# Input tiles of the first down product asked for one row less ahead; sums over features, additions, stores and two rests of weights at other places

## The chip, the cores and the metric

The kernel runs on one core of a Trainium2 chip. The metric is the device time of one execution in microseconds (us); the time before is the median of three executions. Engines are called PE (TensorE, matrix products), ACT (ScalarE), DVE (VectorE), POOL (GpSimd) and SP (SyncE, which here only issues transfers).

## The reference, cut to what matters

One layer of a hybrid block over 1,024 latent tokens of width 1,024, with 256 context tokens: a mixer, and then a SwiGLU network. The change touches the end of the mixer and all of SwiGLU.

```python
D_MODEL, SEQ, CTX_LEN = 1024, 1024, 256
D_FF = 2816                                    # 22 tiles of 128

def rmsnorm(x, g):
    return x * rsqrt(mean(x * x, axis=-1) + 1e-6) * g

def swiglu(h, w_gu, w_down):
    g, u = split(h @ w_gu, 2, axis=-1)
    return (silu(g) * u) @ w_down

y = mixer(rmsnorm(x, g_mix_pre) * (1 + sc_m) + sh_m, ...)
x = x + gt_m * rmsnorm(y, g_mix_post)
h = rmsnorm(x, g_ffn_pre) * (1 + sc_f) + sh_f
x = x + gt_f * rmsnorm(swiglu(h, ffn_w_gu, ffn_w_down), g_ffn_post)
```

All inputs are float32. The kernel keeps that accuracy by splitting each operand into a head (the value rounded to the engine's fp32r format) and a rest (value minus head). A product is then three passes: head by head, head by rest, rest by head.

## The kernel before

Activations lie with features on the 128 partitions and tokens along the row, in two halves of 512 tokens. KT is 8 (tiles of 1,024 features), FT is 22 (tiles of 2,816), NP is 5. A weight tile of 128x1024 is loaded by SP into `raw[:, b]` (b alternates between two buffers). ACT writes its head `w_hi` (line 872, `split` and `head_of`), POOL its rest `w_lo` (line 1363, `rest_of`). These jobs have one numbering through the phases: J_OUT, J_PRE, J_DN, J_D2; `hi_done`, `lo_done` and `job_done` count finished heads, rests and products. A head waits until the product two jobs back is finished (`job_done`), a load until the rest two jobs back is finished (`lo_done`). Each engine takes its instructions strictly in the order written out by hand. SP's order is therefore the order in which transfers are asked for, and a wait in it holds up all later requests.

The phases that matter, in order:

- **Sums over features.** An rmsnorm needs the sum of squares over partitions. DVE adds squares of the 8 tiles into one tile, PE multiplies it with a tile of ones (`sum_over_features(N, acc)`, line 2600; N is 0 to 4), DVE adds epsilon (`variance_of`, line 1992), ACT takes the root (`root`, line 1193), DVE the reciprocal (`inverse_root`, line 1997). Sums 0 and 2 belong to the mixer's output of either half, 1 and 3 to the input of SwiGLU, 4 to the output of SwiGLU for the first half.
- **First products** (J_PRE, `first_half(f, s)`, f = 0 to 21, s = 0 and 1; lines 2656 and 2659). Each f is two half products of 12 matmuls. ACT copies the first out (`first_copy`, line 1234), DVE adds the second to it (`first_sum`, line 2065, into `st2`), and SP stores both to DRAM (`p1_store`, `cg_store`). Meanwhile DVE finishes the second half's mixer output (`add_mixed`), its norm, the scaled input `u1` (line 2124), and prepares four sums of halves (`input_sums`, 2073 to 2078) and their rests (`input_rests`, 2084 and 2086) for the next phase. PE's second half of f waits for `first_sum(f - 2)`, and its first half for `first_copy(f - 2)`.
- **Pair products** (`pair_product(u, r)`, u = 0 to 21, r = 0 to 4; lines 2692 and 2695). Five products of 12 matmuls for each u on sums and differences of weights, which DVE forms (`pair_sums`, lines 2097 to 2102), ACT and POOL split (`pair_head`, `pair_rest`, lines 1257 and 1479). DVE combines the results (lines 2152 to 2177); the gated activations `ab` of both token halves are stored to DRAM in `act_d` (`act_store`).
- **First down product** (J_DN, lines 2716 and 2720), for the first token half. It loops over the 22 rows of `w_down` tiles, i = 0 to 21: row i needs the weight tile `raw` of row i and the activation tile `a0f` of row i, and adds into all 8 banks with 24 matmuls (16 with the head, 8 with the rest of the weight). `rows_dma(i)` loads the weight row (512 KB), `act0_dma(i)` the tile `a0f` (256 KB, two buffers), `act1_dma(i)` the tile `a1f` of the second token half (256 KB, four buffers), which is only split here for later. For each row ACT makes `w_hi`, `a0h` (line 1277) and `a_hi` (1284); POOL makes `w_lo`; DVE makes `a0l` (line 2181) and `a_lo` (2185). PE starts a row on `w_hi` and `a0l`.
- **Second down product** (J_D2, `down_job(k, c)`, lines 2239 and 2244): 8 output tiles k, each of three jobs c. Beside it DVE squares and adds the first half's result (lines 1985 and 1987), then norms it and adds it to x (2198 and 2199); after k = 2 PE waits for that (`n_fin`) and turns it for the output (line 2739). `x1_columns(q)` (line 2759) turns the second half's x.

SP's loop over the rows of the first down product is, before:

```python
for i in range(FT):
    if i + 2 < FT:
        rows_dma(i + 2)          # waits for w_lo of row i
        act1_dma(i + 2)          # from i + 2 = 4: waits for a_lo of row i - 2
        if i + 4 < FT:
            act0_dma(i + 4)      # waits for a0l of row i + 2
```

Of the kernel before, what the change touches and what calls it, by code (L numbers as in the profile page):

```python
# [19 lines left out]
ALU = mybir.AluOpType  # L20
# [27 lines left out]
E_OUT = 0  # L48
# [116 lines left out]
def program(nc, A, out):  # L165
    ctx = ExitStack()
    with ctx:
# [366 lines left out]
        def _(sp):  # L534
# [206 lines left out]
            def rows_dma(i):  # L741

                sp.wait_ge(lo_done, J_DN + i - 1)
                sp.dma_start(raw[:, i % 2, :], w_dn[:, i, :]).then_inc(raw_ld[i % 2], 16)
# [6 lines left out]
            def cg_store(f):  # L751

                sp.wait_ge(c_eva, C_EVA0 + f + 1)
                sp.dma_start(cg_d[f], st2[:, f % 2, :]).then_inc(cg_out[f % 2], 16)
# [31 lines left out]
            def act0_dma(i):  # L786

                if i >= 2:
                    sp.wait_ge(a0_lo, A0_LO0 + i - 1)
                sp.wait_ge(a_out[0], A_OUT0 + 16 * (i + 1))  # L790
                sp.dma_start(a0f[:, i % 2, :], act_d[0, i]).then_inc(a0_ld[i % 2], 16)

            def act1_dma(i):

                if i < 4:
                    sp.wait_ge(a_ok, A_OK0 + 2 * FT)
                else:
                    sp.wait_ge(a1_lo, A1_LO0 + i - 3)
                sp.wait_ge(a_out[1], A_OUT0 + 16 * (i + 1))
                sp.dma_start(a1f[:, i % 4, :], act_d[1, i]).then_inc(a1_ld[i % 4], 16)  # L800
# [3 lines left out]
            sp.wait_ge(n_x1, KT)  # L804
            sp.dma_start(x1_d, x1h[0][:].rearrange("p k n -> p (k n)")).then_inc(x1_out, 16)
            for f in range(FT):
                if f + 2 < FT:
                    gate_dma(f + 2)
                else:
                    rows_dma(f + 2 - FT)  # L810
                p1_store(f)
                if f >= 2:
                    cg_store(f - 2)
                if f in (15, 17):
                    pair_dma((f - 15) // 2)
            cg_store(FT - 2)
# [3 lines left out]
            for u in range(FT):  # L820
                if 1 <= u < FT - 1:
                    first_dma(u + 1)
                if u + 2 < FT:
                    pair_dma(u + 2)
                if u:
                    act_store(u - 1, 1)
                if u in (2, 3):
                    act0_dma(u - 2)
                if u == FT - 1:
                    act0_dma(2)  # L830
                    act0_dma(3)
                act_store(u, 0)
            act_store(FT - 1, 1)
            act1_dma(0)
# [2 lines left out]
            for i in range(FT):  # L837
                if i + 2 < FT:
                    rows_dma(i + 2)
                    act1_dma(i + 2)  # L840
                    if i + 4 < FT:
                        act0_dma(i + 4)
                else:
                    raw_dma(i % 2, J_DN + i + 2, src_d(i + 2 - FT))
                if i in (4, 6, 8, 10):
                    c = (i - 4) * KT * HALF // 8
                    sp.dma_start(x1h[0][:].rearrange("p k n -> p (k n)")[:, c:c + KT * HALF // 4],
                                 x1_d[:, c:c + KT * HALF // 4]).then_inc(x1_ld, 16)
# [17 lines left out]
        def _(act):  # L866
# [369 lines left out]
            def input_sums(j):  # L1236

                for r in (0, 1, 2, 3):
                    act.wait_ge(t_sum, T_SUM0 + 4 * j + r + 1)
                    act.activation(t_hi[r][:, j, :], tsum[:, j % 2, r, :], ACT.Copy).then_inc(th_ok, 1)  # L1240
                act.wait_ge(u_ok, U_OK0 + KT)
                act.activation(t_hi[4][:, j, :], u1[:, 4 + j, :], ACT.Identity, bias=mod[:, 28 + j, 0:1]).then_inc(th_ok, 1)
# [36 lines left out]
            def act1_head(i):  # L1279

                act.wait_ge(a1_ld[i % 4], A1_LD0 + 16 * (i // 4 + 1))
                if i == 0:
# [2 lines left out]

            chain = {1: lambda: root(2), 3: lambda: x1_squares(1, range(1)), 4: lambda: x1_squares(1, range(1, 4)),
                     5: lambda: x1_squares(1, range(4, 8)), 6: lambda: root(3), 10: lambda: input_sums(1),
                     11: lambda: input_sums(2), 12: lambda: input_sums(3)}
            for f in range(FT):
                head_of(J_PRE + f + 1)  # L1290
                if f in chain:
# [67 lines left out]
        def _(pool):  # L1359
# [8 lines left out]
            def rest_of(J):  # L1368
                rest(0, J - J % 2, J % 2)
# [116 lines left out]
            for u in range(FT):  # L1486
                if u:
                    for r in range(NP):
                        pair_rest(u, r)
                if u in (1, 2):  # L1490
                    rest_of(J_DN + u - 1)
            for j in range(2, FT + 24):
                rest_of(J_DN + j)

# [2 lines left out]
        def _(dve):  # L1497
# [543 lines left out]
            def mixed_squares(ks):  # L2041

                for k in ks:
                    dve.wait_ge(acc_free, E_OUT + KT + k + 3)
                    link(dve.tensor_tensor(yacc[:], sq1[:, 0, :] if k == 1 else yacc[:], sq1[:, k, :], ALU.add))

            mixed_squares(range(1, 4))
            rstd_of(1)
            for k in range(KT + 1):
                if k < KT:  # L2050
                    ffn_input(k)
                if k in (1, 2):
                    mixed_squares(range(k + 3, k + 4))
                if k:
                    ffn_rest(k - 1)

# [44 lines left out]
                dve.wait_ge(s_ok, S_OK0 + 4 * u + 3)  # L2101
                dve.tensor_tensor(s4[:], g[:, HALF:D], s2[:], ALU.subtract).then_inc(s_ok, 1)

            mixed_squares(range(6, KT))
            dve.nop().then_inc(n_sum, 1)
            link(dve.tensor_tensor(dsh[:], mod[:, 24:28, 0], mod[:, 28:32, 0], ALU.subtract))
            first_sum(0)
            variance_of(2)
            inverse_root(2)
# [9 lines left out]
            first_sum(5)  # L2119
            variance_of(3)  # L2120
            inverse_root(3)
            first_sum(6)
            for k in range(KT):
                dve.scalar_tensor_tensor(u1[:, k, :], x1h[1][:, k, :], affn[:, k:k + 1], rstd[:], ALU.mult, ALU.mult).then_inc(u_ok, 1)
                if k == 4:
                    first_sum(7)
            input_sums(0)
            first_sum(8)
            input_sums(1)
            first_sum(9)  # L2130
            input_rests(0)
            input_sums(2)
            first_sum(10)
            input_rests(1)
            input_sums(3)
            first_sum(11)
            input_rests(2)
            first_sum(12)
            input_rests(3)
            for f in range(13, FT):  # L2140
                first_sum(f)
                if f == 18:
                    pair_sums(0)
# [87 lines left out]
        def _(pe):  # L2231
# [412 lines left out]
            def first_half(f, s):  # L2644

                b, J, dst = f % 2, J_PRE + f, ps[:, 4 * s + f % 2, :]
                if f >= 2:
                    pe.wait_ge(c_eva if s else p1_ev, (C_EVA0 if s else P1_EV0) + f - 1)
                elif s == 0:
                    pe.wait_ge(acc_free, E_OUT + 16 + 2)  # L2650
                pe.wait_ge(hi_done, J + 1)
                for k in range(4 * s, 4 * s + 4):
                    if f == 0:
                        pe.wait_ge(n_hl, k + 1)
                    for x in (hb_hi, hb_lo):
                        pe.matmul(dst, w_hi[:, b, k * P:(k + 1) * P], x[:, k, :], start=k == 4 * s and x is hb_hi, stop=False)  # L2656
                pe.wait_ge(lo_done, J + 1)
                for k in range(4 * s, 4 * s + 4):
                    ins = pe.matmul(dst, w_lo[:, b, k * P:(k + 1) * P], hb_hi[:, k, :], start=False, stop=k == 4 * s + 3)  # L2659
                ins.then_inc(job_done if s else p1_ps, 1)  # L2660

            x_turns(range(KT, KT + 3))
            for f in range(FT):
                first_half(f, 0)
                if f == 1:
                    sum_over_features(2, yacc)
                if f in (3, 4):
                    x_turns(range(2 * f + 6, 2 * f + 7))
                first_half(f, 1)
                if f in (2, 3, 4):  # L2670
                    x_turns(range(2 * f + 7, 2 * f + 8))
                if f == 5:
                    sum_over_features(3, nrm)

            def pair_product(u, r):
# [94 lines left out]
            for k in range(KT):  # L2770
                for c in range(3):
                    down_job(k, c)
                    if k == 0 and c == 0:
                        pe.wait_ge(y0_a, Y0_A0 + 4)
                        pe.wait_ge(y0_d, Y0_D0 + 4)
                        x1_columns(0)
                        x1_columns(1)
                    if k == 0 and c == 2:
                        sum_over_features(4, nrm)
                if k == 0:  # L2780
                    pe.wait_ge(t_ev, 2)
                    x1_columns(2)
                    x1_columns(3)
                else:
                    pe.wait_ge(t_ev, 4 if k < 5 else 8)
                    down_columns(k - 1)
                if k == 2:
                    pe.wait_ge(n_fin, 1)
                if 2 <= k < 6:
                    if k > 2:  # L2790
                        pe.wait_ge(o_ev, k - 2)
                    output_turns(k - 2)
# [32 lines left out]
```

## Time and profile before

| | us |
|---|---|
| median of three executions | 1476.96 (1475.63 to 1481.14) |
| profiled execution, its time | 1478.04 |
| its span in the trace | 1476.2 |
| PE busy (matmuls) | 1372.9, 93% of the span |
| DVE busy | 954.9, 65% |
| POOL busy | 596.0, 40% |
| ACT busy | 574.2, 39% |
| moved by DMA | 195.73 MB, mean 133 GB/s |

The profiled execution's time is 1.8 us above its span: start and end lie outside the trace. A busy PE means that matmuls are in flight; it can be busy at half its clock. "L2716" is line 2716 of the kernel. "[2.69 <-DVE a0l L2181]" behind an instruction says that its engine was idle for 2.69 us before it, and that DVE's instruction of line 2181 on tile a0l released it. DVEq and PEq stand for an engine's sequencer, SPq for SP's transfer requests.

### The profile page before, as it was taken

What the parts mean: (1) busy time and instruction counts of PE and PEld (TensorE: products, weight loads), DVE (VectorE), ACT (ScalarE), POOL (GpSimd) and SP (SyncE); (2) the same over time, 40 slices, a digit from 0 to 9 for tenths busy, and PEclk for the clock granted to TensorE, in tenths of its full rate; (3) what the DMA queues carried; (4) which work ended last, traced back from release to release, by engine and by line L of the source; (5) the groups of instructions that cost most, each with busy time, mean ns of one, the idle gap of its engine ahead of it and who ended that gap; (6) DMA issues with size and microseconds to landing.
All of it is one profiled execution on the core that took longest, in us unless ns stands there. A gap on an engine that the chain in (4) does not pass through costs nothing.

```text
span 1476.2 us, 19347 instructions
## 1 busy us (share of the span) xinstructions
PE 1372.9 (93%) x7489; PEld 1113.6 (75%) x7489; DVE 954.9 (65%) x1230; ACT 574.2 (39%) x954; POOL 596.0 (40%) x333
## 2 busy tenths in 40 slices
PE   5999998999998999999999999999999776788997
PEld 1589667999887888887777878888888655567886
DVE  6774558884918887459987387777786332346522
ACT  5662653322216778535434422333332222233221
POOL 3363112161428552663433565455552222233442
PEclk9999999999999999999999999999999988899998
DMA  9852113214105445444446745544552434342342
GB/s 324 320 165 64 41 43 103 69 44 142 30 17 140 137 137 145 143 144 141 139 147 205 236 142 157 171 150 143 165 164 77 139 128 141 122 138 68 102 133 87
DMA packets 219910, 195.73 MB, mean 133 GB/s; under 512 B 13043, under 2 KB 179329, under 8 KB 219563
## 3 DMA queue, kind: packets, MB, share of 16 engines
q1 hardware_dynamic: 217827, 187.51, 40.5%
q10 hardware_dynamic: 1992, 6.99, 1.3%
q8 instruction: 59, 0.97, 0.3%
q14 instruction: 32, 0.26, 0.1%
HBM read 160.88 MB, written 33.98 MB: 132 GB/s over the span
## 4 chain that ended last, share of the span: by engine, by line
PE 65%; DVE 17%; DMA 6%; ACT 4%; issue 3%; SPq 1%; POOL 0%; DVEq 0%; ACTq 0%
PE ps L2692 13%; PE ps L2407 11%; PE ps L2695 6%; PE ps L2239 6%; DMA raw<-in_ffn_w_down 6%; PE ps L2412 6%; DVE a0l L2181 3%; PE ps L2244 3%; PE ps L2656 2%; PE ps L2570 2%; PE ps L2547 2%; PE ps L2508 2%; PE ps L2425 1%; PE ps L2659 1%; DVE nrm L2017 1%
## 5 line engine op out<-in xcount | busy, mean ns | idle before, releaser
L1363 POOL TENSOR_TENSOR w_lo<-raw,w_hi 128x1024 fp32r<-128x1024 f32 x84 | 207.8, 2474 | 345.7 <-ACT w_hi L872 345.7
L872 ACT ACTIVATE w_hi<-raw 128x1024 fp32r<-128x1024 f32 x84 | 88.9, 1058 | 254.7 <-DMA raw<-in_ffn_w_down 131.7
L1383 POOL TENSOR_TENSOR w_lo<-raw,w_hi 128x1024 fp32r<-128x1024 f32 x21 | 88.6, 4219 | 219.1 <-ACT w_hi L1017 219.1
L2692 PE MATMUL ps<-t_hi,whi 128*128 128x512 f32 x440 | 171.4, 390 | 3.3 <-DVE ym L2154 3.3
L2692 PE MATMUL ps<-t_lo,whi 128*128 128x512 f32 x440 | 171.2, 389 | 0.0
L1479 POOL TENSOR_TENSOR wlo<-wsum,whi 128x512 fp32r<-128x512 f32 x88 | 123.0, 1400 | 111.9 <-ACT whi L1257 111.9
L2407 PE MATMUL ps<-ha_hi,w_hi 128*128 128x512 f32 (+2 forms) x432 | 162.6, 377 | 3.1 <-ACT p_hy L1024 2.8
L2407 PE MATMUL ps<-ha_lo,w_hi 128*128 128x512 f32 (+2 forms) x432 | 160.3, 371 | 0.0
L2181 DVE TENSOR_TENSOR a0l<-a0f,a0h 128x512 fp32r<-128x512 f32 x20 | 49.0, 2448 | 114.7 <-ACT a0h L1277 114.7
L2716 PE MATMUL ps<-a0h,w_hi 128*128 128x512 f32 x176 | 80.5, 458 | 45.2 <-DVE a0l L2181 45.2
L2695 PE MATMUL ps<-t_hi,wlo 128*128 128x512 f32 x440 | 117.6, 389 | 0.0
L1257 ACT ACTIVATE whi<-wsum 128x512 fp32r<-128x512 f32 x88 | 55.5, 632 | 148.9 <-PE ps L2695 120.1
L2412 PE MATMUL ps<-ha_hi,w_lo 128*128 128x512 f32 (+2 forms) x432 | 99.1, 371 | 0.0
L2692 PEld LDWEIGHTS ps<-t_hi,whi 128*128 128x128 f32 x440 | 82.6, 188 | 21.2 <-DVE ym L2154 4.1
L2695 PEld LDWEIGHTS ps<-t_hi,wlo 128*128 128x128 f32 x440 | 82.6, 188 | 17.1
L2692 PEld LDWEIGHTS ps<-t_lo,whi 128*128 128x128 f32 x440 | 82.6, 188 | 17.1
L2407 PEld LDWEIGHTS ps<-ha_hi,w_hi 128*128 128x128 f32 x432 | 81.1, 188 | 17.1 <-issue 3.2
L2407 PEld LDWEIGHTS ps<-ha_lo,w_hi 128*128 128x128 f32 x432 | 81.1, 188 | 10.2
L2412 PEld LDWEIGHTS ps<-ha_hi,w_lo 128*128 128x128 f32 x432 | 80.0, 188 | 10.3
L2716 PEld LDWEIGHTS ps<-a0h,w_hi 128*128 128x128 f32 x176 | 39.3, 224 | 61.4 <-issue 52.7
L2656 PE MATMUL ps<-hb_hi,w_hi 128*128 128x512 f32 x176 | 73.0, 415 | 6.2 <-DVE st L2065 3.6
L2716 PE MATMUL ps<-a0l,w_hi 128*128 128x512 f32 x176 | 78.2, 444 | 0.0
(348 smaller groups left out, 3029.6 us busy)
## 6 DMA issues: line engine op xcount, KB each, us to landing
raw<-in_ffn_w_gu SPq DMA_DIRECT2D x66, 512.0 KB, 5.6
raw<-in_ffn_w_down SPq DMA_DIRECT2D x38, 512.0 KB, 3.8
ada1x<-in_ada_w SPq DMA_DIRECT2D x32, 512.0 KB, 4.0
raw<-in_w_in SPq DMA_DIRECT2D x22, 512.0 KB, 4.0
act_d<-ab SPq DMA_DIRECT2D x44, 256.0 KB, 2.4
ada<-in_ada_w SPq DMA_DIRECT2D x4, 2048.0 KB, 21.7
raw<-in_w_out SPq DMA_DIRECT2D x16, 512.0 KB, 3.7
p_d<-st SPq DMA_DIRECT2D x22, 256.0 KB, 2.1
```

Source lines behind the costliest of these rows:

```text
L872: act.activation(w_hi[:, b, :], raw[:, b, :], ACT.Copy).then_inc(hi_done, 1)
L1363: pool.tensor_tensor(w_lo[:, b, :], raw[:, b, :], w_hi[:, b, :].bitcast(F32), ALU.subtract).then_inc(lo_done, 1)
L1383: pool.tensor_tensor(w_lo[:, b, :], raw[:, b, :], w_hi[:, b, :].bitcast(F32), ALU.subtract).then_inc(llo, 1)
L1479: pool.tensor_tensor(wlo[r][:], src, whi[r][:].bitcast(F32), ALU.subtract).then_inc(wl_ok, 1)
L2181: dve.tensor_tensor(a0l[:, (i + 1) % 2, :], a0f[:, (i + 1) % 2, :], a0h[:, (i + 1) % 2, :].bitcast(F32), ALU.subtract).then_inc(a0_lo, 1)
L2239: pe.matmul(dst, w_hi[:, b, k * P:(k + 1) * P], x, start=start and i_ == 0 and n == 0, stop=False)
L2407: pe.matmul(dst, w_hi[:, b, k * P:(k + 1) * P], x[:, k, a:z], start=k == 0 and n == 0, stop=False)
L2412: ins = pe.matmul(dst, w_lo[:, b, k * P:(k + 1) * P], ha_hi[:, k, a:z], start=False, stop=k == KT - 1)
L2656: pe.matmul(dst, w_hi[:, b, k * P:(k + 1) * P], x[:, k, :], start=k == 4 * s and x is hb_hi, stop=False)
L2692: pe.matmul(dst, whi[r][:, j * P:(j + 1) * P], x[:, j, :], start=j == 0 and x is t_hi[r], stop=False)
L2695: ins = pe.matmul(dst, wlo[r][:, j * P:(j + 1) * P], t_hi[r][:, j, :], start=False, stop=j == 3)
L2716: pe.matmul(ps[:, m, :], w_hi[:, b, m * P:(m + 1) * P], x[:, b, :], start=i == 0 and x is a0h, stop=False)
```

## The change

Seven edits of order; no instruction of arithmetic is added or removed.

1. In SP's loop over rows of the first down product, `act0_dma(i + 4)` at the end of an iteration becomes `act0_dma(i + 3)` between `rows_dma` and `act1_dma`. `act0_dma(3)` before the loop goes.
2. In the first products SP stores `st2` of f - 2 (`cg_store`) at the start of iteration f, no longer behind `gate_dma(f + 2)` and `p1_store(f)`.
3. POOL makes the rests of weights of rows 0 and 1 of the first down product after the pair products' rests, no longer within u = 1 and u = 2.
4. PE takes sum 3 after f = 6 (before: after f = 5), and sum 4 after job (k = 1, c = 0) (before: after job (k = 0, c = 2)).
5. f = 0 waits for one finished copy of the mixer's output less.
6. DVE adds squares 4 and 5 of the second half, and forms `dsh`, at other places; the sums of inputs and `first_sum` are interleaved otherwise, from f = 6 to 14.
7. ACT takes the heads of input sums 2 and 3 at f = 12 and 14 (before: 11 and 12).

```diff
--- before.py
+++ after.py
@@ -804,13 +804,13 @@
             sp.wait_ge(n_x1, KT)
             sp.dma_start(x1_d, x1h[0][:].rearrange("p k n -> p (k n)")).then_inc(x1_out, 16)
             for f in range(FT):
+                if f >= 2:
+                    cg_store(f - 2)
                 if f + 2 < FT:
                     gate_dma(f + 2)
                 else:
                     rows_dma(f + 2 - FT)
                 p1_store(f)
-                if f >= 2:
-                    cg_store(f - 2)
                 if f in (15, 17):
                     pair_dma((f - 15) // 2)
             cg_store(FT - 2)
@@ -828,7 +828,6 @@
                     act0_dma(u - 2)
                 if u == FT - 1:
                     act0_dma(2)
-                    act0_dma(3)
                 act_store(u, 0)
             act_store(FT - 1, 1)
             act1_dma(0)
@@ -837,9 +836,9 @@
             for i in range(FT):
                 if i + 2 < FT:
                     rows_dma(i + 2)
+                    if i + 3 < FT:
+                        act0_dma(i + 3)
                     act1_dma(i + 2)
-                    if i + 4 < FT:
-                        act0_dma(i + 4)
                 else:
                     raw_dma(i % 2, J_DN + i + 2, src_d(i + 2 - FT))
                 if i in (4, 6, 8, 10):
@@ -1285,7 +1284,7 @@
 
             chain = {1: lambda: root(2), 3: lambda: x1_squares(1, range(1)), 4: lambda: x1_squares(1, range(1, 4)),
                      5: lambda: x1_squares(1, range(4, 8)), 6: lambda: root(3), 10: lambda: input_sums(1),
-                     11: lambda: input_sums(2), 12: lambda: input_sums(3)}
+                     12: lambda: input_sums(2), 14: lambda: input_sums(3)}
             for f in range(FT):
                 head_of(J_PRE + f + 1)
                 if f in chain:
@@ -1487,8 +1486,8 @@
                 if u:
                     for r in range(NP):
                         pair_rest(u, r)
-                if u in (1, 2):
-                    rest_of(J_DN + u - 1)
+            rest_of(J_DN)
+            rest_of(J_DN + 1)
             for j in range(2, FT + 24):
                 rest_of(J_DN + j)
 
@@ -2044,13 +2043,12 @@
                     dve.wait_ge(acc_free, E_OUT + KT + k + 3)
                     link(dve.tensor_tensor(yacc[:], sq1[:, 0, :] if k == 1 else yacc[:], sq1[:, k, :], ALU.add))
 
-            mixed_squares(range(1, 4))
+            mixed_squares(range(1, 5))
+            link(dve.tensor_tensor(dsh[:], mod[:, 24:28, 0], mod[:, 28:32, 0], ALU.subtract))
             rstd_of(1)
             for k in range(KT + 1):
                 if k < KT:
                     ffn_input(k)
-                if k in (1, 2):
-                    mixed_squares(range(k + 3, k + 4))
                 if k:
                     ffn_rest(k - 1)
 
@@ -2101,9 +2099,8 @@
                 dve.wait_ge(s_ok, S_OK0 + 4 * u + 3)
                 dve.tensor_tensor(s4[:], g[:, HALF:D], s2[:], ALU.subtract).then_inc(s_ok, 1)
 
-            mixed_squares(range(6, KT))
+            mixed_squares(range(5, KT))
             dve.nop().then_inc(n_sum, 1)
-            link(dve.tensor_tensor(dsh[:], mod[:, 24:28, 0], mod[:, 28:32, 0], ALU.subtract))
             first_sum(0)
             variance_of(2)
             inverse_root(2)
@@ -2119,25 +2116,27 @@
             first_sum(5)
             variance_of(3)
             inverse_root(3)
-            first_sum(6)
             for k in range(KT):
                 dve.scalar_tensor_tensor(u1[:, k, :], x1h[1][:, k, :], affn[:, k:k + 1], rstd[:], ALU.mult, ALU.mult).then_inc(u_ok, 1)
                 if k == 4:
-                    first_sum(7)
+                    first_sum(6)
+            first_sum(7)
             input_sums(0)
             first_sum(8)
             input_sums(1)
             first_sum(9)
             input_rests(0)
+            first_sum(10)
             input_sums(2)
-            first_sum(10)
+            first_sum(11)
             input_rests(1)
+            first_sum(12)
             input_sums(3)
-            first_sum(11)
+            first_sum(13)
             input_rests(2)
-            first_sum(12)
+            first_sum(14)
             input_rests(3)
-            for f in range(13, FT):
+            for f in range(15, FT):
                 first_sum(f)
                 if f == 18:
                     pair_sums(0)
@@ -2647,7 +2646,7 @@
                 if f >= 2:
                     pe.wait_ge(c_eva if s else p1_ev, (C_EVA0 if s else P1_EV0) + f - 1)
                 elif s == 0:
-                    pe.wait_ge(acc_free, E_OUT + 16 + 2)
+                    pe.wait_ge(acc_free, E_OUT + 16 + f + 1)
                 pe.wait_ge(hi_done, J + 1)
                 for k in range(4 * s, 4 * s + 4):
                     if f == 0:
@@ -2669,7 +2668,7 @@
                 first_half(f, 1)
                 if f in (2, 3, 4):
                     x_turns(range(2 * f + 7, 2 * f + 8))
-                if f == 5:
+                if f == 6:
                     sum_over_features(3, nrm)
 
             def pair_product(u, r):
@@ -2775,7 +2774,7 @@
                         pe.wait_ge(y0_d, Y0_D0 + 4)
                         x1_columns(0)
                         x1_columns(1)
-                    if k == 0 and c == 2:
+                    if k == 1 and c == 0:
                         sum_over_features(4, nrm)
                 if k == 0:
                     pe.wait_ge(t_ev, 2)
```

## Rows read from the trace of the kernel before

**Rows 1.** Stretches: us; busy time of PE, PEld, DVE, ACT, POOL; clock; DMA share; GB/s.
```profile
788.00:837.00 49.00, 47.94 (x203) 39.23 (x204) 20.52 (x24) 19.87 (x27) 26.47 (x13) 0.97 0.78 240
...
1151.00:1327.00 176.00, 130.80 (x483) 100.81 (x481) 63.92 (x43) 43.67 (x64) 48.99 (x21) 0.88 0.39 130
```

**Rows 2.** PE's waits from 600 us on: waiter, releaser, us in total, times, longest.
```profile
PE ps L2716 <- DVE a0l L2181: 45.2, 18, 5.0
PE ps L2600 <- DVEq L2118: 5.0, 1, 5.0
PE ps L2600 <- DVEq L2193: 4.2, 1, 4.2
...
PE ps L2692 <- DVE ym L2154: 3.3, 2, 1.6
```

**Rows 3.** Timeline of all engines, one row of the first down product: start, us, what.
```profile
1153.38 0.42 SPq L744 DMA_DIRECT2D raw<-in_ffn_w_down  x1
...
1157.36 1.06 ACT L872 ACTIVATE w_hi<-raw 128x1024 fp32r<-128x1024 f32 x1 [6.33 <-DMA raw<-in_ffn_w_down]
...
1158.49 2.35 POOL L1363 TENSOR_TENSOR w_lo<-raw,w_hi 128x1024 fp32r<-128x1024 f32 x1 [6.06 <-ACT w_hi L872]
...
1158.97 2.42 DVE L2181 TENSOR_TENSOR a0l<-a0f,a0h 128x512 fp32r<-128x512 f32 x1 [5.39 <-ACT a0h L1277]
...
1161.42 0.32 SPq L791 DMA_DIRECT2D a0f<-act_d  x1
...
1161.54 0.77 PE L2716 MATMUL ps<-a0h,w_hi 128*128 128x512 f32 x1 [2.69 <-DVE a0l L2181]
```

**Rows 4.** Timeline of PE: starts of rows 0, 1 and 2, and the end.
```profile
1140.44 0.39 PE L2716 MATMUL ps<-a0h,w_hi 128*128 128x512 f32 x1
...
1145.88 0.39 PE L2716 MATMUL ps<-a0h,w_hi 128*128 128x512 f32 x1
...
1153.12 0.47 PE L2716 MATMUL ps<-a0h,w_hi 128*128 128x512 f32 x1 [1.64 <-DVE a0l L2181]
...
1326.95 0.39 PE L2720 MATMUL ps<-a0h,w_lo 128*128 128x512 f32 x1
```

**Rows 5.** Transfers from 1140 to 1330 us: count, KB each, median us to landing.
```profile
raw<-in_ffn_w_down SPq DMA_DIRECT2D x22, 512.0 KB, 3.9
a1f<-act_d SPq DMA_DIRECT2D x22, 256.0 KB, 4.1
a0f<-act_d SPq DMA_DIRECT2D x18, 256.0 KB, 2.7
```

**Rows 6.** Timeline of PE in the first products.
```profile
740.09 2.07 PE L2600 MATMUL ps<-nrm,ones 128*128 128x512 f32 x2 [4.96 <-DVEq L2118]
...
788.51 0.50 PE L2656 MATMUL ps<-hb_hi,w_hi 128*128 128x512 f32 x1 [2.77 <-DVE st L2065]
...
836.43 1.07 PE L2659 MATMUL ps<-hb_hi,w_lo 128*128 128x512 f32 x4
```

**Rows 7.** Timeline of DVE in the pair products.
```profile
853.61 2.88 DVE L2097 TENSOR_TENSOR wsum<-raw 128x512 f32<-128x512 f32 x1
...
859.45 0.67 DVE L2152 TENSOR_TENSOR px<-px,ps 128x512 f32<-128x512 f32 x1
```

**Rows 8.** Timeline of POOL, pair products and start of the first down product.
```profile
857.29 4.61 POOL L1479 TENSOR_TENSOR wlo<-wsum,whi 128x512 fp32r<-128x512 f32 x3 [1.35 <-ACT whi L1257]
...
1150.06 2.37 POOL L1363 TENSOR_TENSOR w_lo<-raw,w_hi 128x1024 fp32r<-128x1024 f32 x1 [21.01 <-ACT w_hi L872]
```

**Rows 9.** Timeline of PE in the second down product.
```profile
1342.89 1.52 PE L2244 MATMUL ps<-a_hi,w_lo 128*128 128x512 f32 x6
...
1356.69 1.98 PE L2244 MATMUL ps<-a_hi,w_lo 128*128 128x512 f32 x8
...
1384.23 1.09 PE L2739 MATMUL ps<-ident,x1a 128*128 128x128 f32 x8 [0.16 <-DVEq L2200]
```

**Rows 10.** Timeline of DVE in the second down product.
```profile
1360.38 3.35 DVE L1997 RECIPROCAL rstd<-nrm 128x512 f32<-128x512 f32 x1 [9.44 <-ACT nrm L1193]
```

## The prediction

> **What bounds the kernel now.** I read the page first: PE has the most busy time, but a share over the whole span hides stages. So next came the windows by stage. In the first down product (1151 to 1327 us) PE is busy for only 130.80 of 176 us, at a granted clock of 0.88, while DMA works 39% of its time; in the first products just before (788 to 837 us) PE is nearly always busy, at 0.97 [rows 1]. Then the list of PE's waits: 45.2 us go to `a0l` of DVE in that stage, and four smaller sums elsewhere are touched by the diff [rows 2]. The chain of waits names, in that stage, the same three things again and again: the load of `raw`, `a0l`, the load of `raw`. Last, the timeline of one row shows why [rows 3].
>
> There the reader should see one closed loop. SP asks for the weight tile at 1153.38. ACT starts its head at 1157.36, DVE's `a0l` runs from 1158.97 to 1161.39, and only at 1161.42 does SP go on, with the request for `a0f`; the next weight tile comes right behind it. SP stands at `act0_dma(i + 4)`, which waits for `a0l` of row i + 2, and that row's weights were asked for only in the same iteration. So a weight tile is requested, carried, split and used before the next is requested: one in flight, though there are two buffers. Rows 0 and 1, prefetched, follow each other after 5.44 us (1140.44 to 1145.88). From the start of row 2 to the end of row 21 PE needs 1153.12 to 1327.2, so 174.1 us for 20 rows, 8.70 each [rows 4].
>
> **The first down product.** After the change iteration i asks for weights i + 2, then `a0f` of i + 3, which waits for `a0l` of row i + 1. That row's weights were requested one iteration earlier. The loop stays, but now it spans two rows. Its length: landing, then the 4.2 us from ACT's head to PE's start (1157.36 to 1161.54) [rows 3]. The landing grows, because the request for a weight tile now stands behind `a0f` and `a1f`. Before, the last of the same three requests, `a1f`, starts about 0.9 us after the first and lands in 4.1 us: 5.0 us for the 1 MB [rows 5]. With that, two rows take at least 5.0 + 4.2 = 9.2 us, 4.6 each. That is below PE's 5.44, so PE becomes the bound. Second loop: a head waits for the product two rows back, and 4.2 us later its row is ready, while PE works 5.44 us on the row between; 1.2 us are left. ACT's three splits, DVE's two and POOL's one take at most 3.1 us a row, hidden under 5.44. Moved past each other on SP: `a1f` now stands behind the wait for `a0l`, but has four buffers and is not needed by PE here. Four iterations also load 512 KB of x; a landing 1.7 us longer would make that pair of rows 10.9 us, just PE's 10.88, so I cost it at nothing in the sum and at 5 us in the range.
>
> Bandwidth: 1.05 MB in 5.44 us is 193 GB/s; 788 to 837 us moves 240 GB/s for 49 us with PE hardly waiting [rows 1].
>
> Row 2's start stays as it is, since its weights are asked for behind the stores of the last activations, in the same place as before. So 20 rows x 5.44 = 108.8, plus 0.4 for its slow clock: 109.2 instead of 174.1. **Gain 64.9 us.**
>
> On the length of a transfer, the Trainium skill ("DMA: Bandwidth & Descriptors", section "Anatomy of one DMA") fits, for transfers that GpSimd issues, about 2.0 us plus bytes over 436 GB/s. An estimate by that page for the 1 MB would be 4.4 us; the rows give 5.0 for requests of SP, and I use the rows. By either, PE stays the bound and the sum is the same.
>
> **The first products.** PE waits 4.96 us for sum 3 and starts it at 740.09, so the sum's input was ready then [rows 6]. The idle began at 735.13; f = 6, put in the gap, takes 5.44 and ends at 740.6, so the sum finds its input ready and DVE's chain behind it loses nothing. The whole price is larger than the idle: from 735.1 to the end of f = 21 (837.5) PE takes 102.4 us for 16 x 5.44 + 0.9 (the sum) = 87.9 of work, a loss of 14.5. It holds the 4.96, a wait for `first_sum` (2.77 at 788.51) [rows 6] and matmuls at half clock behind these. What comes back: `first_sum(6)` now stands behind five tiles of `u1`. I count sum 0.9, root and reciprocal 4.7, five tiles and the addition 6 with one stall: it is done near 751, when PE, at f = 8, would want it at 749.5: 1.4 us. From there DVE does sums or rests, 3.0 us, an addition, 0.6, and one stall of 2.1 behind POOL (2.88 less 0.7 to 0.8) per f, about 5.7 against PE's 5.44, over eight f: 2 us less a slack of 1. I give back 2.5. Squares, `dsh` and the earlier start of f = 0 move things by under 1 us either way; `cg_store` first only blocks SP if `first_sum(f - 2)` is later than PE's first half of f - 1, and then `gate_dma(f + 2)` and `p1_store(f)` wait behind it; with a load needed 10 us later, cost nothing. I add 0.5 for f = 0. **Gain 12.5 us** (bounds: 5, when most of the idle comes back at f = 8 to 16; 15, when none does).
>
> **The pair products.** In u = 1 and 2 POOL works on a rest of 128x1024 while DVE wants two inputs from SBUF: L2097 takes 2.88 us, where `px`, with as many elements, takes 0.67 [rows 7], and PE waits 3.3 us for `ym` [rows 2]. Without these rests, with the slow matmuls behind each wait: **gain 3.7 us**. The two rests go into POOL's idle time before 1150.06, 21.01 us long [rows 8]. They take 2.4 us each, from 1129.05 to 1133.8, and are needed at 1144 by the tail of row 0; without that cover they would cost 4.8. DVE combines u = 21 at that time. It need not suffer: `px` took 0.67 us at 859.45 inside POOL's 4.61 us stretch from 857.29 [rows 7, 8]. That instruction has one input in PSUM.
>
> By the Trainium skill ("SBUF — State Buffer", section "Who interferes with whom"), DVE and GpSimd block each other when DVE reads two inputs from SBUF, and not with at most one. The trace agrees, 2.88 against 0.67 us. If every DVE instruction were blocked, PE would wait some 0.3 us in u = 21, and the sum would be 0.3 smaller.
>
> **The second down product.** PE waits 4.2 us for the input of sum 4 [rows 2]. Job 2 ends at 1344.3 and job 3 at 1358.5, 14.2 us [rows 9], for a sum (0.9), 16 transposes (1.8) and a job (5.44), 8.1 at full clock. With the sum last, the wait is filled. Is the chain behind it late? No: the root stood in ACT's queue behind the head that waits for job 3, so the reciprocal started at 1360.38, after an idle of 9.44 us [rows 10], though the sum was long done. Afterwards it starts 0.9 (sum) + 1.6 (epsilon, root) after job 3, not 1.9: so 0.6 later after job 3. But PE, too, now has the sum (0.9) between job 3 and its wait for `n_fin`, which was 0.16 us [rows 9] and doesn't grow; it rises by up to 2 us if one more DVE instruction falls under one of POOL. **Gain 6.0 us.**
>
> **Sum.** 64.9 + 12.5 + 3.7 + 6.0 = 87.1, from 1478.04 (span 1476.2 and 1.8 around it): 1390.9. The profiled execution was 1.1 above the median, so 1390.
>
> **Rivals.**
> - *Carriage is late (10%).* If a weight tile behind two others lands after 8.5 us, not 5.0, two rows take 12.7, 6.35 each: 18 us less gain, 1408. For it: x's loads, and ACT's head waiting 6.33 us for landings now. Against: 240 GB/s was held.
> - *DVE becomes late in the first products (10%).* Most of the idle comes back at f = 8 to 16 (the bound of 5 in place of 12.5) and the chain to `n_fin` adds 2: 9.5 us less, 1399. For it: 5.7 us of DVE against 5.44 of PE per f. Against: before, the same work had one wait of PE of 2.77 us for it [rows 6].
> - *The request does not help (4%).* Were the row's 8.70 us set by something other than SP's wait, only the other parts count: 22.2 us, 1455. Against: SP resumes 0.03 us after `a0l` [rows 3].
> - *Transfers of one queue go one after another (2%), slower.* A row then needs 3.9 + 2.7 + 4.1 = 10.7 us [rows 5], 40 us more over 20 rows, less 22.2: 1495. It decides from 9.8 us a row on. Against: the three are requested within 0.9 us and have all landed after 5.0.
>
> By the Trainium skill ("DMA: Bandwidth & Descriptors", section "Queues, rings and completion order"), descriptors of one ring start in order and a later one may complete before an earlier one; it speaks against the last rival, and the trace agrees.
>
> **Chances.** My forecast 0.74; the rivals 0.10, 0.10, 0.04, 0.02. They give 1390, 1408, 1399, 1455, 1495. The range reaches to 1405 and down to 1384 (no idle given back, f = 0 starting earlier, median lower). Within 0.5% is about what a measurement of this kernel can tell from no change: 0.01; slower 0.02; faster 0.97.
>
> **What would show it.** Right: about 5.44 us from row to row, SP asking for `a0f` while the weights of the next row are in flight, ACT waiting for PE and not for landings, clock 1.00 there; sum 3 and sum 4 without idle before them; no long L2097 in u = 1 and 2. Wrong: ACT's heads still wait for `raw`; rows above 6 us; new waits of PE for `first_sum` at f = 8 to 16; a wait for `n_fin` of several us.

## The result and the profile after

| | median us (lowest to highest) | runs |
|---|---|---|
| before | 1479.05 (1475.63 to 1483.78) | 4 |
| after | 1408.08 (1403.66 to 1411.31) | 4 |
| ratio | 0.9516, 95% interval 0.9473 to 0.9559 | |

The kernel became 4.8% faster, some 71 us. I had forecast 1390 with a range of 1384 to 1405, so the gain came, but smaller than the range allows: the median lies 18 us above the forecast. The profiled execution of after took 1403.66 us, 74.4 less than that of before (the forecast for this pair was 87.1); the working below is made between these two.

The stretches of the profile after that answer to [rows 1] (us; busy time of PE, PEld, DVE, ACT, POOL; clock; DMA share; GB/s):

```profile
786.00:835.00 49.00, 43.38 (x184) 35.14 (x183) 25.62 (x27) 18.91 (x27) 23.42 (x12) 0.97 0.71 221
1146.00:1259.00 113.00, 109.57 (x479) 89.64 (x480) 64.21 (x43) 43.70 (x63) 49.54 (x21) 1.00 0.59 198
```

The first down product now has PE busy for 97% at a clock of 1.00, where it was 74% at 0.88. The stretch of the first products before it, which had looked full, is now the poorer one: 43.38 of 49 us.

PE's waits after, which answer to [rows 2]:

```profile
PE ps L2655 <- ACT w_hi L871: 5.6, 1, 5.6
PE ps L2655 <- DVE hb_lo L2026: 2.7, 6, 0.6
PE ps L2715 <- DVE a0l L2180: 2.4, 3, 1.7
PE ps L2599 <- DVEq L2103: 1.8, 1, 1.8
PE ps L2715 <- ACT w_hi L871: 1.3, 1, 1.3
PE ps L2655 <- DVE st L2063: 0.9, 1, 0.9
```

The 45.2 us for `a0l` are 2.4, and the waits for sums 3 and 4 and for `ym` are gone. Three waits have no counterpart before: 5.6 us for a head of weights in the first products, 1.8 for sum 2, and 1.3 for a head of weights at row 13 of the first down product. The 2.7 us for `hb_lo` stand where 2.5 for `yo` stood, at the start of f = 0.

One row of the first down product in the profile after, SP, ACT and DVE, against [rows 3]:

```profile
1225.62 0.32 SPq L791 DMA_DIRECT2D a0f<-act_d  x1
1226.03 0.38 SPq L800 DMA_DIRECT2D a1f<-act_d  x1
1226.46 0.42 SPq L744 DMA_DIRECT2D raw<-in_ffn_w_down  x1
```
```profile
1226.94 1.06 ACT L871 ACTIVATE w_hi<-raw 128x1024 fp32r<-128x1024 f32 x1 [3.34 <-PE ps L2719]
```
```profile
1228.55 2.48 DVE L2180 TENSOR_TENSOR a0l<-a0f,a0h 128x512 fp32r<-128x512 f32 x1 [2.36 <-ACT a0h L1276]
```

The reader should compare two things with before. ACT's head here no longer waits for the load but for PE's product two rows back (so do 14 of 21 heads from row 2 on; the heads of rows 2, 3, 7, 9, 11, 13 and 14 still wait for their load). And it starts 0.5 us after a request for weights, so it cannot be using that tile: its own was asked for earlier. The end of row 21 follows the start of row 2 (1147.43) after 111.9 us, 5.59 a row.

Where the 74.4 us came from, stage by stage in the two profiles. A stage begins and ends with an instruction that both have:

| stretch | before | after | gain | forecast |
|---|---|---|---|---|
| start to the turn of x ahead of f = 0 | 693.27 | 694.95 | -1.7 | 0 |
| from there to the first pair product | 144.1 | 140.5 | 3.5 | 12.5 |
| pair products | 303.1 | 299.2 | 3.9 | 3.7 |
| rows 0 and 1 of the first down product | 12.7 | 12.8 | -0.1 | 0 |
| rows 2 to 21 | 174.1 | 111.9 | 62.2 | 64.9 |
| second down product, to the end | 149.0 | 142.6 | 6.4 | 6.0 |

The hole is in the first products: 9.0 of the 12.7 us that this execution lacks.

### The profile page after: what moved, and what is told of

It reads as the page before. It is cut to its first block, busy times and chain, and to the rows that moved or that the text cites. A ratio compares the mean times of both kernels' runs of the same rounds, so it can differ in the third digit from the quotient of the medians.

```text
span 1401.9 us, 19347 instructions
## 1 busy us (share of the span) xinstructions
PE 1345.7 (96%) x7489; PEld 1098.0 (78%) x7489; DVE 955.8 (68%) x1230; ACT 572.9 (41%) x954; POOL 596.2 (43%) x333
## 4 chain that ended last, share of the span: by engine, by line
PE 77%; DVE 11%; ACT 4%; issue 2%; DMA 2%; SPq 0%; DVEq 0%; ACTq 0%
PE ps L2691 14%; PE ps L2406 12%; PE ps L2238 8%; PE ps L2694 7%; PE ps L2411 6%; PE ps L2243 4%; PE ps L2715 3%; PE ps L2655 3%; PE ps L2569 2%; DMA raw<-in_ffn_w_down 2%; PE ps L2719 2%; PE ps L2546 2%; PE ps L2507 1%; PE ps L2658 1%; PE ps L2424 1%
## 5 line engine op out<-in xcount | busy, mean ns | idle before, releaser
L2715 PE MATMUL ps<-a0h,w_hi 128*128 128x512 f32 x176 | 68.9, 392 | 3.7 <-DVE a0l L2180 2.4
L2238 PE MATMUL ps<-a_hi,w_hi 128*128 128x512 f32 x176 | 69.9, 397 | 0.0
L1443 POOL TENSOR_TENSOR tb<-gt,mask 128x288 f32<-128x288 f32 (+1 forms) x48 | 52.6, 1125 | 39.8 <-DVE amin L1957 38.3
```

The costliest lines, as they stand in the source:

```text
L2238: pe.matmul(dst, w_hi[:, b, k * P:(k + 1) * P], x, start=start and i_ == 0 and n == 0, stop=False)
L2715: pe.matmul(ps[:, m, :], w_hi[:, b, m * P:(m + 1) * P], x[:, b, :], start=i == 0 and x is a0h, stop=False)
```

## The experiments

The runs came in three groups, and each group timed the kernel before beside them. Medians of one kernel differ by up to 2.5 us between groups, so a kernel is set against others of its group where it can be.

**First group: what each part is worth, and what stands behind PE's new wait.** The timelines of after around that wait, SP, ACT, PE and DVE:

```profile
794.55 0.60 SPq L749 DMA_DIRECT2D p_d<-st  x1
802.98 1.01 SPq L765 DMA_DIRECT2D raw<-in_ffn_w_gu  x2
804.03 1.03 SPq L754 DMA_DIRECT2D cg_d<-st  x1
805.10 0.43 SPq L560 DMA_DIRECT2D raw<-in_ffn_w_gu  x1
```
```profile
811.05 1.06 ACT L871 ACTIVATE w_hi<-raw 128x1024 fp32r<-128x1024 f32 x1 [10.94 <-DMA raw<-in_ffn_w_gu]
```
```profile
812.25 0.77 PE L2655 MATMUL ps<-hb_hi,w_hi 128*128 128x512 f32 x1 [5.62 <-ACT w_hi L871]
```
```profile
800.07 2.88 DVE L2084 SCALAR_TENSOR_TENSOR t_lo<-u,mod,t_hi 128x512 fp32r<-128x512 f32 x1
```

Read it from below: PE waits for ACT's head, the head for a load, and the load was asked for late. DVE's last rest of the input sums ends at 802.95. Only then does SP send L765, the first request of weights for the pair products (`pair_dma(0)`), which stands after f = 15 and waits for exactly these rests. Behind it in SP's order stand a store and, at 805.10, the weights of f = 18 (L560). They travel behind 1 MB, so ACT gets them at 811.05 and PE stands for 5.62 us. SP's waits name it: 

```profile
SPq L765 <- DVE t_lo L2084: 7.8, 1, 7.8
```

The kernel before has no such wait. The same rest and the same request there:

```profile
796.56 2.88 DVE L2086 SCALAR_TENSOR_TENSOR t_lo<-u,mod,t_hi 128x512 fp32r<-128x512 f32 x1
```
```profile
802.79 1.21 SPq L765 DMA_DIRECT2D raw<-in_ffn_w_gu  x2
```

The last rest was finished at 799.44, 3.3 us before SP came to the request.

E1, the changed kernel again, as the mark. 

> The changed kernel again, unaltered, as the mark for the other runs of this call. If the spread of its four runs so far (1403.7 to 1411.3) belongs to the kernel, its median lies near 1408 and single runs differ by several us; if the runs above 1410 were chance of the chip, it lies near 1404.

Measured: 1406.03 us (1403.48 to 1408.49), ratio to before 0.9504 (0.948 to 0.9528). Single runs differ by 5 us, as those of the kernel before in this group do (1477.11 to 1482.39). PE's waits for `a0l` are 5.1 us in this profile against 2.4, and rows 0 to 21 take 126.3 us against 124.6: a part of the spread lies in that stage.

E2, the kernel before with the first edit alone:

```diff
-                    act1_dma(i + 2)
-                    if i + 4 < FT:
-                        act0_dma(i + 4)
+                    if i + 3 < FT:
+                        act0_dma(i + 3)
+                    act1_dma(i + 2)
```

> The kernel before with one edit: a0f of row i + 3 asked for ahead of a1f of row i + 2 (and no a0f of row 3 before the loop). Theory: this edit carries nearly the whole gain, 62 us as the traces of before and after show for this stage: 1415 to 1419, PE 112 us from row 2 to the end of row 21. Rival (the stage's gain came with the other edits, which moved the phase of the engines to one another): less than 50 us, above 1427.

Measured: 1416.98 us, ratio 0.9589 (0.956 to 0.9618), 61.8 us less than before in the same group, of the 72.8 of E1. This edit carries most of the gain by itself, and PE's waits for `a0l` are 4.8 us in its profile.

E3, the changed kernel without that edit. 

> The changed kernel with the request of a0f as before (one row more ahead, at the end of an iteration). Theory: what is left is the pair products (3.8), the second down product (6.5) and about 3.7 of the first products, 14 us: 1463 to 1467. Rival (the other edits are worth 22 us, as I predicted, and the first down product is what fell short): 1455 to 1458.

Measured: 1466.07 us, ratio 0.9917 (0.9893 to 0.994), 12.7 us less than before. The rest of the diff is worth 13 us, not the 22 of my forecast, and its profile has the same 5.6 us of waiting for a head. So the hole is not in the first down product.

E4, the changed kernel with the pair requests two products later:

```diff
-                if f in (15, 17):
-                    pair_dma((f - 15) // 2)
+                if f in (17, 19):
+                    pair_dma((f - 17) // 2)
```

> The changed kernel with the two requests of weights for the pair products after f = 17 and 19, not 15 and 17. Theory: PE's 5.6 us before f = 18 come from SP standing at the first of them until the last rest of the input sums is there (802.87), with the weights of f = 18 asked for behind it. Then the wait and its slow matmuls go: 7 us less than the changed kernel in the same call, SP's wait for t_lo 0 to 1 us. Rival (the transfers of 1 MB themselves hold up the weights of f = 18, wherever they stand): the same wait of about 5 us of PE two products later, at f = 20, and no change beyond 1 us.

Measured: 1398.26 us (1394.97 to 1398.79), ratio 0.9444 (0.9422 to 0.9466), 7.8 us less than E1. SP's timeline and PE's waits in E4:

```profile
804.65 1.79 SPq L765 DMA_DIRECT2D raw<-in_ffn_w_gu  x2
...
808.60 0.43 SPq L560 DMA_DIRECT2D raw<-in_ffn_w_gu  x1
```
```profile
PE ps L2715 <- DVE a0l L2180: 4.1, 3, 2.8
PE ps L2655 <- DVE hb_lo L2026: 2.7, 6, 0.6
PE ps L2599 <- DVEq L2103: 1.9, 1, 1.9
PE ps L2655 <- DVE st L2063: 0.9, 1, 0.9
```

The same 1 MB stands in the same way ahead of the weights of f = 20, but the request doesn't wait, and PE has no wait for a head. So it was the wait in SP's queue, not the transfer: the rival is out.

**Second group: the other parts one by one.** E5, the kernel before with sum 3 after f = 6 (`if f == 5` becomes `if f == 6`). 

> The kernel before with one edit: sum 3 after f = 6. Theory: PE's 5.0 us of waiting for it go, with the slow matmuls behind: 6 to 7 us less, near 1472. PE, now earlier, may wait longer for first_sum at f = 9 to 14, where DVE's order is still the old one: 2.8 us there could become up to 8, and then little is gained (1476 to 1479). Rival: the idle is the sum's own price, and moves with it to f = 7.

Measured: 1472.79 us, ratio 0.9958 (0.9942 to 0.9973), 6.9 us less. The wait of 5.0 is gone, and it doesn't reappear; PE's waits for `first_sum` are 4.0 us, as against 3.6 before. The feared growth didn't come. From the turn of x to the first pair product PE takes 138.4 us, 5.7 less than before.

This run also tells something about SP's wait. PE is earlier here, but DVE's order is the old one, and SP does not wait at the pair request:

```profile
794.40 2.88 DVE L2086 SCALAR_TENSOR_TENSOR t_lo<-u,mod,t_hi 128x512 fp32r<-128x512 f32 x1
```
```profile
799.75 1.63 SPq L765 DMA_DIRECT2D raw<-in_ffn_w_gu  x2
```

Counted from the turn of x ahead of f = 0 (693.27 before, 696.51 in E5, 694.95 after), the last rest ends at 106.2, 100.8 and 108.0 us, and SP comes to the request at 109.5, 103.2 and 100.2. With sum 3 moved, PE and the rests come earlier together, and no wait arises; against E5 the changed kernel has SP 3.0 us earlier and, by its new order of DVE's work, the rests 7.2 us later.

E6, the kernel before with sum 4 after job (k = 1, c = 0) and the two rests of weights behind the pair products. 

> The kernel before with two edits far apart: sum 4 after job (k = 1, c = 0), and the rests of weights of rows 0 and 1 behind the pair products. Theory: 6.0 to 6.5 us in the second down product and 3.7 in the pair products, 10 us: 1468 to 1469, no wait of PE for the input of sum 4, none for ym, the wait for n_fin under 1 us. Rival (the norm behind sum 4 is later by the 5.4 us of a job and PE stands at n_fin): 1473 or more, a wait of about 5 us at the turn of x.

Measured: 1468.16 us, ratio 0.9924 (0.9907 to 0.994), 11.6 us less by medians (10.8 between the two profiled spans). DVE and PE there, against [rows 9, 10]:

```profile
1349.63 3.35 DVE L1997 RECIPROCAL rstd<-nrm 128x512 f32<-128x512 f32 x1 [0.70 <-ACT nrm L1193]
```
```profile
1373.50 1.04 PE L2739 MATMUL ps<-ident,x1a 128*128 128x128 f32 x8
```

The reciprocal had waited 9.44 us for the root; now 0.70. PE turns x without a wait before it: a sum one job later did not make the norm late.

E7, E4 with squares 4 and 5 at their old places (`dsh` stays early):

```diff
-            mixed_squares(range(1, 5))
+            mixed_squares(range(1, 4))
...
+                if k in (1, 2):
+                    mixed_squares(range(k + 3, k + 4))
...
-            mixed_squares(range(5, KT))
+            mixed_squares(range(6, KT))
```

> The kernel with pair requests after f = 17 and 19, and DVE's squares 4 and 5 of the second half back at their old places (4 and 5 inside the loop over ffn_input, 6 and 7 behind it); dsh stays early. Theory: of the first products' missing gain 2 us lie in the squares: three of them behind the loop meet two rests of POOL, and sum 2 waits 1.9 us. Then the sum's input is ready 2 us earlier, PE's wait for it is under 0.5 us, and the whole is 1.5 to 2.5 us shorter. Rival: the delay is that of the chain ahead of the loop (one square and dsh more before the root), or of PE's clock after its early start at f = 0: then the wait stays, and nothing is gained or some is lost.

Measured: 1397.16 us (1394.35 to 1398.96), ratio 0.9447 (0.9433 to 0.9461); against 1398.26 in another group that shows nothing by itself, and E8 below, of this group and without this edit, is no slower (1396.54). The times alone do not show a gain; the profiles do. From the turn of x ahead of f = 0 to the first pair product E4 takes 133.5 us and E7 131.0, and PE has no wait for sum 2. From that turn to sum 2 all five profiles without this edit (after, E1, E3, E4, E8) take 15.9 to 16.0 us, and all five with it (E7 and E9 to E12) 13.6 or 13.7. DVE and POOL in after, and DVE in E7:

```profile
704.51 6.27 DVE L2044 TENSOR_TENSOR yacc<-yacc,sq 128x512 f32<-128x512 f32 x3
```
```profile
704.76 5.47 POOL L1362 TENSOR_TENSOR w_lo<-raw,w_hi 128x1024 fp32r<-128x1024 f32 x2 [8.30 <-ACT w_hi L871]
```
```profile
702.93 3.49 DVE L2044 TENSOR_TENSOR yacc<-yacc,sq 128x512 f32<-128x512 f32 x2
```

Three additions left for the end fall on two rests of POOL back to back, and take 6.27 us for 2.1 of work; of two left for the end, one is held up, and they take 3.49.

E8, E4 with the four loads of x in iterations 4, 8, 12 and 16 (slices as before). 

> The kernel with pair requests after f = 17 and 19, and the four loads of x (512 KB each) in iterations 4, 8, 12 and 16 of the first down product, not 4, 6, 8 and 10. Theory: four loads two rows apart fall on the weights of rows of the same parity, the loop over two rows is then over 10.9 us long, and PE waits for a0l near rows 7 to 13; four rows apart each delay is made good before the next. PE's waits for a0l go from 4.1 us to the 1.7 to 2.8 at row 2, 1.5 to 2.5 us less. Rival: the waits come from transfers as such: the same waits, further apart.

Measured: 1396.54 us (1393.9 to 1400.06), ratio 0.9444 (0.9426 to 0.9462): no difference from E4 that these runs can tell. My expectation that only the wait at row 2 would be left was wrong: 3.4 us in all, of which 1.75 at row 2; behind it 1.6 in four waits, where E4 has 1.3 in two. The four waits are at rows 7, 11, 15 and 19, whose weights are the next request behind a load of x. Each load of x has its wait, further apart. The rival holds.

**Third group: the length of the burst.** The mark is E7 again. 

> The kernel with pair requests after f = 17 and 19 and squares 4 and 5 at their old places, unaltered, as the mark for the other three of this call: about 1396, PE 124 to 126 us from the start of row 0 to the end of row 21 of the first down product (22 rows at 5.44 are 119.7).

Measured: 1394.68 us (1392.78 to 1398.34), 123.3 us for the 22 rows in the profile, 1.6 us of waits for `a0l` and 1.3 for a head. The same kernel as E7 had 126.2 us and 5.3 us of waits for `a0l`, so one profile of this stage is no measure of 2 or 3 us.

E10, the mark with the loads of x behind weights 2 to 5 of the second down product. 

> The mark with the four loads of x asked for in the second down product (one behind each of the weights 2 to 5), none in the first. Theory: without x a weight tile lands 6.0 us after the first of its three requests, the loop over two rows is 10.2 us, under PE's 10.88, and PE has no wait for a0l behind row 2; the stage takes about 122 us, 3 to 4 less than the mark. Rival: transfers are late without x too, and PE's waits for a0l stay above 3 us; or the loads of x now come too late for the norm's end, and a wait for n_fin of several us takes the gain.

Measured: 1392.05 us (1390.61 to 1393.96), ratio 0.9405 (0.9389 to 0.942). PE's waits in this stage:

```profile
PE ps L2717 <- DVE a0l L2182: 2.7, 1, 2.7
```

It is the one at row 2. The waits behind it are gone, and rows 3 to 21 take 5.44 us each, PE's own time; so they do in E11 and E12. In E9 these rows take 2.1 us more and in E7 4.6 more. Transfers without x are in time. But the stage as a whole is no shorter than the mark's (124.2 us, and about 123.5 in E11 and E12), where I had expected 122. Row 2 started 1.4 us later after row 0 than in the mark, and then ran slowly:

```profile
1139.20:1146.27 7.07, 7.07 (x24) 5.73 (x25) 3.83 (x3) 0.44 (x1) 2.08 (x1) 0.77 0.78 266
```

The granted clock in it is 0.77; in the mark row 2 takes 5.56 us at 1.00. E4, E11 and E12 have the slow row 2 too (7.1 us), E1, E2, E7 and E8 don't. Why is open: E1 waited 2.3 us just before a quick row 2, E11 only 1.9 before a slow one. By medians 2.6 us are gained; the ranges overlap.

E11, the mark with `act1_dma(i + 2)` ahead of `act0_dma(i + 3)`. 

> The mark with a1f of row i + 2 asked for ahead of a0f of row i + 3, so ahead of SP's wait for a0l. Theory (position within the iteration matters only through the length of the burst): a1f goes out earlier, the burst behind the wait is 0.75 MB, not 1 MB, weights land 0.8 us sooner after the wait, and PE's waits for a0l fall from 5.3 to 2 to 4 us: 1 to 3 us less. Rival: the place ahead of a1f is what the gain needs; then rows take longer than 5.44 us and the whole is several us more.

Measured: 1393.09 us (1392.3 to 1393.54), ratio 0.9416 (0.94 to 0.9432). PE waits 1.9 us for `a0l`, at row 2 alone, and a load of weights takes 4.4 us at the median, not 5.0. So `a0f` asked for one row less ahead is what counts; its place ahead of `a1f` isn't needed. By medians the new place is worth 1.6 us, with ranges that overlap.

E12, both. 

> The mark with both edits: loads of x in the second down product, and a1f ahead of a0f. Theory: the two are one cure for the same lateness, so this is no better than the better of them by more than 1 us: about 1392 to 1394, PE's only wait for a0l that at row 2. Rival (they add): 3 us below either.

Measured: 1392.21 us (1391.87 to 1394.24), ratio 0.9412 (0.9396 to 0.9429), as expected no better than either. These three are the best versions run, some 14 us below the changed kernel's 1406.03 of another group; they are not told apart by these runs.

## Why the prediction was right and wrong

**The first down product: right in mechanism, 2.7 us off in size.** One tile in flight was the limit, and PE became the bound. The mis-sized term is x: "I cost it at nothing in the sum". What went before it was the landing. I put "5.0 us for the 1 MB", from `a1f`, which stood last. After, the weights stand last; transfers of the profile after, against [rows 5]:

```profile
raw<-in_ffn_w_down SPq DMA_DIRECT2D x22, 512.0 KB, 5.1
a1f<-act_d SPq DMA_DIRECT2D x22, 256.0 KB, 3.2
a0f<-act_d SPq DMA_DIRECT2D x19, 256.0 KB, 2.8
```

From the first request (1225.62) to that for weights pass 0.84 us, and 5.1 more to the landing: 5.9, so a loop over two rows of 10.1 instead of 9.2. That is still under 10.88 and costs nothing by itself, but it leaves 0.8 us, where I had counted on 1.7. The four tiles asked for right behind a load of x (rows 7, 9, 11 and 13) landed after 7.0, 5.9, 5.7 and 7.0 us, and PE waited 0.47, 0.23, 0 and 1.30 us at these rows. With the slower matmuls behind the waits, rows 3 to 21 take 3.0 us more than 5.44 each. E10 to E12 show that this goes in either of two ways: x elsewhere, or fewer bytes ahead of the weights.

**The first products: the step that failed.** "Gain 12.5 us (bounds: 5, when most of the idle comes back at f = 8 to 16; 15, when none does)" became 3.5, below my lower bound. The parts I looked at came as worked out: sum 3 has no idle before it and its edit alone gives 6.9 us (E5); PE's one wait for `first_sum`, at f = 8, is 0.9 us, for which I had given back 1.4; f = 9 to 16 have no wait, for which I had given back 1. I had compared DVE with PE alone. What I left out is another reader of DVE's work: `pair_dma(0)` in SP's queue waits for the last of the input rests. Before, SP came to it 3.3 us after they were done (802.75 against 799.44). After, SP came to it at 795.15, 7.6 us earlier, and the rests were done at 802.95, 3.5 us later; SP stood for 7.8 us, with the weights of f = 18 behind it. Two things met. PE, and with it SP, ran ahead. And two more additions (f = 13 and 14) stand ahead of the last rest, so that DVE's work is spread over more of POOL's rests: eight of its instructions from the first input sum on take 2.9 us, where E5, in the old order, has five. E5 also shows that the first of the two is not enough for a wait. Which of edits 2, 6 and 7 is needed was not run. I had said for `cg_store` what stands behind it in SP's queue, but not asked which other waits there would now be late. E4 settles what the wait cost: 7.0 us in the stage, 7.8 in the median.

The second error is "Squares, `dsh` and the earlier start of f = 0 move things by under 1 us either way". The squares cost 2.5 us of this stage (133.5 in E4, 131.0 in E7), by falling on two rests of POOL. The price of one such stall stood in [rows 7]; I didn't ask how many the moved additions would meet. Together 9.5 us, where 9.0 were missing; with both mended (E7) the stage gains 13.1 us over before, for 12.5 in the forecast.

**Pair products** (3.9 for 3.7) and **second down product** (6.4 for 6.0) were right, E6 with both, and so was the reason: the root stood in ACT's queue, not behind the sum. The two rests fit into POOL's idle time, and `px` of u = 21 kept its 0.69 us.

**The rest** up to the median: this execution spent 1.7 us more ahead of f = 0, where PE's work is the same, and the median of its kernel is 4.4 us above it. E1 came to 1406.03. The median of before rose too, from 1476.96 to 1479.05 with its fourth execution. The executions of either kernel spread over 8 us, and so 4.4 us between one of them and their median is nothing special.

Of the rivals, "Carriage is late" named a real effect at a sixth of its size; "DVE becomes late" came near in size (9.5 us less; 9.0 were missing), but by luck: DVE was late for SP's queue and not for PE, and a part of the loss was the squares. The argument against it was also a little off: before has two waits of PE for `first_sum` in that stretch, 0.85 and 2.77 us, not one. The request did help (E2), and rows took 5.6 us, not the 10.7 of serial transfers.

## What to carry to other kernels

When work of one engine is made earlier and of another later, list every wait in every queue on the later work, SP's first: a request that waits holds back all later ones, and what it costs is known only from what stands behind it. A weight tile is asked for in time only if no wait on its own predecessor's use lies between two requests; count the loop over all buffers, with the landing of the tile that is last in the burst, and with the occasional transfers that stand in front of it. And when additions are collected at one place, look how many of POOL's instructions they will meet there, if they read two tiles of SBUF.

## What was not expected of the hardware

The same 512 KB tile of weights lands after 3.9 us (median, profile before) with 256 KB requested just ahead of it, and after 5.1 with 512 KB (profile after). From row 4 on, the tiles of the profile after without a load of x in front land after 4.8 to 5.9 us, those with one after 5.7 to 7.0.

The kernel before, E2, E5 and E6 have equal code in all engines up to the turn of x ahead of f = 0, and reach it after 693.05 to 696.51 us: 3.5 us of difference before the first edited instruction counts, as much as most single edits here are worth. Over all profiles of this study it is 692.8 to 696.5.
